# Row work of a two-block layer: half of three residual additions on GpSimd, weight parts reordered, closing products by halves

## The reference

```
mix = concat(attn, rec) @ w_out ;  h = h + rmsnorm(mix, g_post_mix)   # seam 1
u = rmsnorm(h, g_pre_ffn) ;        f = square(relu(u @ w_ff1)) @ w_ff2
h = h + rmsnorm(f, g_post_ffn)                                        # seam 2
u = rms_norm(h, ln_pre_mix) ;      proj = u @ w_in   (attention, delta rule, gates)
h = h + rms_norm(merged @ w_out, ln_post_mix)                         # seam 3
f = rms_norm(h, ln_pre_ffn) ;      f = (silu(f @ gate) * (f @ up)) @ down
h = h + rms_norm(f, ln_post_ffn)                                      # seam 4
out = h + sigmoid(h @ w_ple_gate) * rms_norm(p @ w_ple, ln_ple)
```

## Time and profile before

| quantity | value |
|---|---|
| median of three runs | 973.11 us |
| the profiled execution, its own time | 973.03 us |
| its span, first to last instruction | 970.9 us |
| TensorE matmul busy | 904.8 us, 93% |
| VectorE busy | 604.5 us, 62% |
| ScalarE busy | 525.1 us, 54% |
| GpSimd busy | 18.5 us, 2% |
| mean granted TensorE clock | 0.977 |

### The profile page before, as it was taken

One profiled execution on the slowest core, in us unless ns is written; L12 is line 12 of the kernel. 1 busy time (PEld: TensorE's weight loads), 2 busy tenths in 40 slices (PEclk: granted clock), 3 DMA queues, 4 the chain that ended last, 5 costly groups with the idle time before them and its releaser, 6 DMA issues.

```text
span 970.9 us, 16760 instructions
## 1 busy us (share of the span) xinstructions
PE 904.8 (93%) x6490; PEld 842.1 (87%) x6490; DVE 604.5 (62%) x967; ACT 525.1 (54%) x908; POOL 18.5 (2%) x34
## 2 busy tenths in 40 slices
PE   4997879999999799999999999999997999999977
PEld 4984669999998799999899989898986999999956
DVE  4576475555555676669677777755757545555455
ACT  5486464544445755666556564835457444444443
POOL 1000030000000000000000000000000000000000
PEclk9998979999999899999999999999999999999979
DMA  9731257555656254554213141324554565565601
GB/s 309 260 131 44 87 95 244 188 175 189 198 178 204 75 178 150 169 165 139 88 53 123 44 130 43 131 81 137 180 208 145 177 210 175 183 204 175 229 31 44
DMA packets 106941, 144.90 MB, mean 149 GB/s; under 512 B 2968, under 2 KB 94360, under 8 KB 106896
## 3 DMA queue, kind: packets, MB, share of 16 engines
q1 hardware_dynamic: 104608, 137.60, 43.2%
q0 software_dynamic: 1968, 6.02, 2.3%
q10 hardware_dynamic: 320, 0.66, 0.2%
HBM read 143.22 MB, written 1.05 MB: 149 GB/s over the span
## 4 chain that ended last, share of the span: by engine, by line
PE 79%; DVE 10%; ACT 7%; issue 2%; DMA 1%; ACTq 0%; DVEq 0%
PE ps L1624 15%; PE ps L1626 14%; PE ps L1625 14%; PE ps L1630 8%; PE ps L1632 8%; PE ps L1631 8%; PE ps L1966 2%; PE ps L1953 2%; DVE wl L1085 2%; PE ps L1970 2%; DVE R L1370 2%; ACT wh L574 1%; DVE R L1122 1%; PE ps L1775 1%; DVE h L1128 1%
## 5 line engine op out<-in xcount | busy, mean ns | idle before, releaser
L1085 DVE TENSOR_TENSOR wl<-w_raw,wh 128x1024 fp32r<-128x1024 f32 x258 | 313.8, 1224 | 243.3 <-ACT wh L574 242.4
L1624 PE MATMUL ps<-xTh,wh 128*128 128x256 f32 (+1 forms) x1160 | 336.4, 290 | 4.2 <-DVE xTl L1112 4.2
L1625 PE MATMUL ps<-xTl,wh 128*128 128x256 f32 (+1 forms) x1160 | 327.9, 283 | 0.0
L1626 PE MATMUL ps<-xTh,wl 128*128 128x256 f32 (+1 forms) x1160 | 327.8, 283 | 0.0
L574 ACT ACTIVATE wh<-w_raw 128x1024 fp32r<-128x1024 f32 x258 | 270.9, 1052 | 99.7 <-PE ps L1632 75.3
L1624 PEld LDWEIGHTS ps<-xTh,wh 128*128 128x128 f32 x1160 | 220.9, 190 | 7.7 <-DVE xTl L1112 3.9
L1625 PEld LDWEIGHTS ps<-xTl,wh 128*128 128x128 f32 x1160 | 220.5, 190 | 1.9 <-issue 1.0
L1626 PEld LDWEIGHTS ps<-xTh,wl 128*128 128x128 f32 x1160 | 221.0, 191 | 0.0
L1630 PE MATMUL ps<-wh,y 128*128 128x512 f32 x224 | 89.5, 400 | 4.0 <-DVE y L1574 4.0
L1632 PE MATMUL ps<-wh,y 128*128 128x512 f32 x224 | 88.8, 396 | 0.0
L1631 PE MATMUL ps<-wl,y 128*128 128x512 f32 x224 | 88.5, 395 | 0.0
(11 more groups left out here) (338 smaller groups left out, 1256.7 us busy)
## 6 DMA issues: line engine op xcount, KB each, us to landing
w_raw<-in_w_in_dram SPq DMA_DIRECT2D x43, 1024.0 KB, 5.0
w_raw<-in_w_ff_dram SPq DMA_DIRECT2D x32, 1024.0 KB, 5.5
w_raw<-in_w_ffn_gate_dram SPq DMA_DIRECT2D x11, 1024.0 KB, 5.1
w_raw<-in_w_ffn_up_dram SPq DMA_DIRECT2D x11, 1024.0 KB, 5.2
w_raw<-in_w_ffn_down_dram SPq DMA_DIRECT2D x11, 1024.0 KB, 4.8
w_raw<-in_w_out_dram SPq DMA_DIRECT2D x8, 1024.0 KB, 4.9
w_raw<-in_w_proj_a_dram SPq DMA_DIRECT2D x4, 1024.0 KB, 5.0
w_raw<-in_w_proj_b_dram SPq DMA_DIRECT2D x4, 1024.0 KB, 4.8
```

The costliest lines, as they stand in the source:

```text
L1085: TT(split_view(wl, pu % UNITS, layout), raw_unit(SLOT[p], j, layout), split_view(wh, pu % UNITS, layout).bitcast(F32), ALU.subtract).then ...
L1624: mm(out, wh_, xh, start=first, stop=False)
L1625: mm(out, wh_, xl, start=False, stop=False)
L1626: return mm(out, wl_, xh, start=False, stop=last)
```

## The change

The additions of the first 512 columns in seams 1 to 3 go to GpSimd (`first_halves`), with two new semaphores: `hp_scaled` from VectorE to GpSimd, `hp_ready` back to VectorE and ScalarE. `h_ready` is then raised twice in these seams, four times in seam 4. Some `hi` and `lo` calls move behind the row work, one table preload goes, one moves up, and `acc_tail` takes the last two units half by half.

```diff
+            def first_halves(n):
+                for t in range(NT):
+                    pool.wait_ge(hp_scaled, 2 * n + t + 1)
+                    pool.tensor_tensor(h[:, t, 0:512], h[:, t, 0:512], u[:, t, 0:512], ALU.add).then_inc(hp_ready, 1)
             for n in range(2, 5):
                 gain_free(n)
                 pool.dma_start(gain[:, n % 2, :], ...
+                if n == 2:
+                    first_halves(0)
+            first_halves(1)
             pool.wait_ge(h_ready, 4)
             ...                       (the eight loads of small2)
             for n in range(5, 9):
                 ...
+                if n == 6:
+                    first_halves(2)
@@ rows_root
-                    act.wait_ge(h_ready, 4 * n + 2 * t + half + 1)
+                    act.wait_ge(h_ready if half else hp_ready, 2 * n + t + 1)
@@ ScalarE, seam 1
             sums_root(0, 0, 21)
+            sums_root(0, 1, 21)
+            rows_root(0, 0)
             hi(22)
-            hi(23)
-            rows_root(0, 0)
-            sums_root(0, 1, 21)
+            rows_root(0, 1)
             piece_hi(0)
             piece_hi(1)
-            rows_root(0, 1)
-            hi(24)
+            hi(23)
             piece_hi(2)
             piece_hi(3)
+            hi(24)
             hi(25)
@@ ScalarE, seam 2
-            act.preload_act_table(ACT.Sqrt)
             sums_root(1, 0, F + 63)
             sums_root(1, 1, F + 63)
-            hi(F + 66)
             rows_root(1, 0)
             rows_root(1, 1)
             for n in range(4):
                 piece_hi(n)
+            hi(F + 66)
             hi(F + 67)
@@ ScalarE, seam 3
             merged_hi(3)
+            act.preload_act_table(ACT.Sqrt)
             for n in range(6):
                 hi(2 * P_OUT2 + n + 4)
...
-            act.preload_act_table(ACT.Sqrt)
             sums_root(2, 0, 2 * P_OUT2 + 7)
             sums_root(2, 1, 2 * P_OUT2 + 7)
+            rows_root(2, 0)
+            rows_root(2, 1)
             hi(2 * P_FF2)
-            rows_root(2, 0)
-            hi(2 * P_FF2 + 1)
-            rows_root(2, 1)
             piece_hi(0)
             piece_hi(1)
+            hi(2 * P_FF2 + 1)
             ple_rows(0)
@@ add_rows
+                shared = g < 7
                 for half in range(2):
                     ins = STT(u[:, t, cols_], acc[:, 2 * t + half, :], ...
+                    if shared and half == 0:
+                        ins.then_inc(hp_scaled, 1)
+                        continue
@@ norm_rows
                 inverse(8 + 4 * t + 3, of=nst)
+                dve.wait_ge(hp_ready, 2 * (g // 2) + t + 1)
@@ VectorE, seam 1
             add_rows(1, 0)
+            add_rows(1, 1)
+            norm_rows(1, 0)
+            norm_rows(1, 1)
+            for n in range(2):
+                piece_lo(n)
             lo(22)
-            norm_rows(1, 0)
-            add_rows(1, 1)
-            piece_lo(0)
-            piece_lo(1)
-            norm_rows(1, 1)
-            piece_lo(2)
-            piece_lo(3)
+            for n in range(2, 4):
+                piece_lo(n)
@@ VectorE, seam 3
             norm_rows(5, 0)
+            norm_rows(5, 1)
             lo(2 * P_FF2)
-            norm_rows(5, 1)
@@ acc_tail
+                end = len(pus) - 1
+                order = [(n, half) for n in range(end - 1) for half in range(2)] + [(n, half) for half in range(2) for n in (end - 1, end)]
                 for t in range(NT):
-                    for n, (pu, (xh, xl)) in enumerate(zip(pus, xs)):
+                    for n, half in order:
@@ seam 4
-            transposes(h, h_ready, 12)
+            transposes(h, h_ready, 6)
```

More of the change, by code:

```diff
@@ L369, in build @@
         ut_hi, ut_lo = sem("uT_hi_ready"), sem("uT_lo_ready")
-        h_ready = sem("h_ready")
+        h_ready, hp_ready, hp_scaled = sem("h_ready"), sem("h_first_half_ready"), sem("first_half_scaled")
         v1_out = sem("v1_ready")
@@ L1676, in acc_tail @@
             def acc_tail(pus, xs, last_=True, opens=False):
+                end = len(pus) - 1
+                order = [(n, half) for n in range(end - 1) for half in range(2)] + [(n, half) for half in range(2) for n in (end - 1, end)]
                 for t in range(NT):
-                    for n, (pu, (xh, xl)) in enumerate(zip(pus, xs)):
-                        if t == 0:
+                    for n, half in order:
+                        pu, (xh, xl) = pus[n], xs[n]
+                        if t == 0 and half == 0:
                             unit_ready(pu)
                         a, b = wh[:, pu % UNITS, :], wl[:, pu % UNITS, :]
[L1683 to L1689, removed]
+                        last = three_tok(acc[:, 2 * t + half, :], xh[:, t * P:(t + 1) * P], xl[:, t * P:(t + 1) * P],
+                                         a[:, half * 512:(half + 1) * 512], b[:, half * 512:(half + 1) * 512], False,
+                                         n == end, group=False)
+                        if n == end and 2 * t + half < 3:
+                            last.then_inc(rows_done, 1)
+                        if t == 1 and half == 1:
                             last.then_inc(unit_done, 1)
```

## The result

| quantity | before | after |
|---|---|---|
| median, on the same chip | 972.28 us (971.25 to 975.59, 6 runs) | 979.89 us (977.81 to 980.80, 6 runs) |
| ratio, with its 95% interval | | 1.0071 (1.0052 to 1.0089) |
| profiled execution: time, span | 973.03, 970.9 us | 979.95, 977.8 us |
| mean granted TensorE clock | 0.977 | 0.968 |

The kernel became slower by 7.6 us (0.71%). The forecast was 4.5 us slower; the time lies inside the range, and nearest to rival A, the slow landing.

A forecast was written before the change was run, and what follows sets the result against it. TensorE was taken as the bound nearly everywhere (79% of the span), a seam costing its standstill. Terms +1.2 + 6.7 - 2.7 - 0.7 = +4.5 on 973.03 gave 977.5 us, range 971.5 to 982.0.

The forecast's parts named there:

- rival A: After seam 2 the late small loads land in 8.3 us, not 5.5: 980.3 us in all; chance 0.22.
- seam 1: VectorE's low part of a weight unit now delays TensorE's products, 134.45 against 133.22: +1.2 us (0.6 to 1.4).
- seam 2, and the loads behind it: Small loads issued late, landing in 5.5 us: gate products +4.7, half clock +2.0, together +6.7 us (2.5 to 9.6).
- seam 3: Earlier preload, sooner first bank and shorter tiles give -1.8, clock staying up counted half: -2.7 us (-1.4 to -4.0).
- end: At the last sigmoids and additions, the first bank completes one triple sooner: -0.7 us (0 to -0.7).
- the reorder gains nothing up to here: In seam 1, reordered row work ends VectorE's scalings at 131.25, where they ended at 131.29 before.
- The GpSimd addition: In the seams it takes 1.1 us and VectorE's last addition waits for it: a tile 2.75 us, not 2.96.

The follow-up runs named there:

- E1: The changed kernel with the eight small loads issued early again, after seam 1, all else of the change kept: 971.49 us, ratio 0.9983 to the kernel before.

## Why the prediction was right, and where it was off

Sign and mechanism were right, and the time lies in the range. The forecast difference was 3.1 us short (4.5 against 7.6): the landing took more than the 5.9 us from which rival A decides, and 1.9 us came in places that no step had, 1.4 of them with a fall of the clock. Some agreements are luck in part, as told below. The terms:

| step | predicted | found |
|---|---|---|
| seam 1 | +1.2 | +0.6 |
| seam 2, and the loads behind it | +6.7 | 7.14 - 1.04 + 1.71 = +7.8 |
| seam 3 | -2.7 | -2.9 |
| end | -0.7 | -0.6 |
| not foreseen: clock, elsewhere | 0 | +1.9 |
| sum | +4.5 | +6.8 in the profiles, +7.6 in the medians |

**Seam 1 (+1.2, found +0.6).** The step "the reorder gains nothing up to here" was off. VectorE finished its scalings at 131.27, when the lag ahead of the seam was already +0.44, so the row work had gained 0.46. The rest, the low part of unit 22 in the path for its 1.2 us, was nearly as predicted: from the scalings' end to the start of the products it took 2.99 us in place of 1.93, 1.06 more. That the start itself agrees, 134.26 with a forecast of 134.45, is partly the 0.44. Putting the low part back gave 0.78.

**Seam 2 and the loads (+6.7, found +7.8).** Seam 2 itself gained as forecast: 1.04 - (-0.16) = 1.2 between the products after seam 1 and the first unit behind seam 2, of which about 0.2 was clock regained (the lag had fallen to +0.82 by 309) and 0.98 the seam. The order of events held: h_ready reaches 4 late, issues, landing, ScalarE, VectorE, TensorE. Two sizes were off. The last issue came at 327.50 and not 326.6: the last addition ended at 319.55 where 318.86 was forecast, with the 0.82 us of lag brought along; the first issue came 0.30 us after it (0.09 forecast), and the eight issues took 7.65 us (7.62 forecast). And the landing was 7.1 us and not 5.5. That is the mis-sized term, 1.6 us: past the 5.9 from which rival A decides. I had weighed the empty DMA engines at 320 to 322 against the 8.3 us of the earlier trace rows and let them pull the value down. But it was the group's own loads that filled the engines. The standstill lasted 5.66 us (5.8 forecast), but this agreement is luck: it ended 2.4 us later than forecast (335.32, not 332.9), and it also began 2.6 us later (329.66, not 327.1). Of these 0.7 are the later start of the first unit (324.70, where 324.86 - 0.85 = 324.01 was forecast), and 1.85 are its length, 4.96 us in place of 3.11, at half clock. The forecast had it at full clock; the late landing hid the loss. Behind the standstill the clock was half as forecast: 8.85 - 7.14 = 1.71 us, against 2.0.

The Trainium skill, "DMA: Bandwidth & Descriptors", section Rules for kernel authors, says that a strided last dimension becomes one descriptor for each element. The trace agrees in kind: conv_w_2 brings the DMA engines to 0.83 busy at 6 GB/s. The price for a load that queues behind such ones comes from the runs: 6.0 us against 3.0, and 7.1 against 3.4.

**The GpSimd addition.** Taken as 1.1 us, it is 1.27; a tile was taken as 2.75 us from its reciprocal to the next and is 2.77 in seam 2. Here two errors cancel: VectorE's addition ends 0.54 us after GpSimd's, and not the whole 0.69. The choice that VectorE's addition waits was right, and the side addition showed why. That without the wait the time would be about 1 us less does not follow from the prediction's own numbers: 0.45 us for each of two tiles, in seams 2 and 3, are 1.8. The Trainium skill, "SBUF — State Buffer", section Who interferes with whom, says that a VectorE instruction with two SBUF inputs contends with a GpSimd instruction that reads SBUF, and not with one that only writes it. The runs agree: 0.69 becomes 1.00 to 1.23 with a reading GpSimd, and stays 0.69 beside a memset.

**Seam 3 (-2.7, found -2.9).** The first reciprocal came 3.24 us after the copy and not 4.28, a gain of 1.04 where 1.5 was forecast. Two tiles gave 0.4, as said. TensorE stood 2.63 us (2.3 forecast) and its clock stayed up, which I had counted by half, as 0.8: from the first reciprocal to the products it took 13.02 us and not 14.86, of which 0.4 are the tiles and 1.44 the clock (0.65 on the transposes alone). The two errors cancelled, which is luck. This term is not a firm one: E1 and the change both take these 13.02 us, while the kernels with loads turned round and with unit 22 moved take 14.34 and 14.62 with the same row work. The first of these stood only 2.27 us and had its clock down; the second stood 2.63 us, exactly as E1 and the change, and its clock fell where theirs stayed up. So the length of the standstill does not settle it; what does stayed open.

**The end (-0.7, found -0.6)** was right: 1.79 in place of 2.43 us.

**What no step had.** +0.44 us were there before any changed instruction had run. That is no effect of the change: the same copy stands at 109.25 in E1 and at 111.37 in the kernel with unit 22 moved. Another +1.40 came between 378 and 727 with the same instructions (at 673.04, below, the lag is still 8.77), and 0.1 behind seam 3. A stretch of 20 us shows the 1.40, the changed kernel's and then that of before:

```profile
660.00:680.00 20.00, 17.71 (x138) 17.54 (x137) 9.02 (x14) 10.45 (x20) 0.00 (x0) 0.91 0.53 172
```

```profile
660.00:680.00 20.00, 17.71 (x148) 17.54 (x147) 12.38 (x19) 10.90 (x13) 0.00 (x0) 1.00 0.49 160
```

The granted clock is 0.91 where it was 1.00, with TensorE equally busy. In this stretch TensorE stands still once, equally long in both, here again the changed kernel first:

```profile
673.04 0.36 PE L1639 MATMUL ps<-yTh,wh 128*128 128x256 f32 x1 [2.29 <-DVE R L1533]
```

```profile
664.27 0.35 PE L1624 MATMUL ps<-yTh,wh 128*128 128x256 f32 x1 [2.29 <-DVE R L1518]
```

Behind it the clock is half from about 673.6 to 677 in the changed kernel, and stays up in the kernel before. All twelve kernels have this standstill of 2.29 us. Behind it the clock falls in seven, E1 and the one with late loads alone among them, and stays up in five: before the change, without sharing, in the first kernel with unit 22 moved, with the old closing order, and in the one with GpSimd's side addition, while it falls in the one with the memset. So neither the late loads nor a later arrival explain it (E1 comes to this place 1.07 us before the kernel before, at 663.20); why it falls stayed open.

**The whole.** The kernel with late loads alone is 9.9 us slower, the change without them gains 1.5; together 8.4, and measured were 7.6, with intervals of up to 1.9 us either way.

## What to carry to other kernels

A wait or a computation put into an engine's instruction order delays every DMA issue written behind it, so before work moves to an engine that "only loads", list its later issues and who first needs them. Where loads must be late, issue first what is needed first, and give loads of single elements a semaphore of their own: here that order alone was worth the same as issuing them 190 us earlier. Handing half of a two-input addition to GpSimd buys little when VectorE's own additions from SBUF then wait for it.

## What the runs showed of the hardware

- A two-input addition of 128x512 float32 takes GpSimd 1.27 us and VectorE 0.69. Where they overlap they take turns: 1.77 to 1.79 for GpSimd when it comes second, 1.00 to 1.23 for VectorE when it does. VectorE's scaling with one input in PSUM (0.75) and its additions beside a memset (0.69) are not touched.
- Four loads of 12 KB in 4-byte elements take GpSimd 5.7 us to issue, and loads of 64 KB behind them land 6.0 and 7.1 us after their issue; ahead of them they take 3.0 and 3.4.
- A standstill of 5.66 us left the clock at half and cost 1.7 us afterwards; in seam 3, standstills of 2.27 us in one kernel and 2.63 in another ended with the clock down in the first and up in the second. A standstill of 2.29 us at one and the same place left the clock up in five kernels and was followed by its fall in seven.
